# A hybrid attention, recurrence and expert layer: output projection by token block, an earlier first and second choice of experts

## The chip, the core and the metric

One core of a Trainium2 chip runs the whole layer once. The metric is the device time of one execution in microseconds (us). The engines are TensorE (PE, with its weight loads as PEld), VectorE (DVE), ScalarE (ACT), GpSimd (POOL) and the queue engine SyncE (SP). Sixteen DMA engines move data between HBM and the on-chip memory. A kernel is a list of instructions for each engine; engines meet at semaphores, and each engine runs its own list strictly in order.

## The reference

All numbers are 32-bit. There are 256 tokens of width 2048 (`SEQ`, `D_MODEL`), one layer.

```
h = x * (1.0 + scale1) + shift1
y = hybrid_mixer(h, ...)      # attention || gated recurrence, merged by gates, then @ w_out
x = layer_norm(DEEPNORM_ALPHA * x + (1.0 + gate1) * y, ln1_g, ln1_b)
h = x * (1.0 + scale2) + shift2
y = peer_ffn(h, peer_wq, peer_subkeys, peer_u, peer_v)
x = layer_norm(DEEPNORM_ALPHA * x + (1.0 + gate2) * y, ln2_g, ln2_b)

# peer_ffn, per token and head (8 heads):
q = h @ w_q;  half_scores = q . sub_keys           # two halves of 128 keys
s_top, i_top = top_k(half_scores, 16)              # then the best 16 of the 16 x 16 sums
act = x . u_tab[expert];  w = softmax(best) * gelu(act);  out = sum w * v_tab[expert]
```

So each token needs, in each of 8 heads, 16 rows of `u_tab` and 16 rows of `v_tab` (8 KB each) that depend on its own data.

## The kernel before

**Data.** Tokens are in two blocks of 128 (block 0, block 1). Weights come in chunks of 256 columns, [128, 4096] numbers (2048 KB), into four slots of `arena` called `ring[0..3]`. `stream` loads them in a fixed rotation on SP's queue. PSUM has eight banks.

**Until the output projection.** Attention, the recurrence and eight rounds of merging gates run on PE from the start to about 844 us. The last round leaves `merged_t`, the input of the output projection.

**Output projection (L884 with `merged_t`).** For each of eight weight chunks, PE multiplies both token blocks (64 recorded matmuls a chunk). Between chunks it broadcasts the adaLN rows (`spread_mod_rows`, L1039, L1035). DVE adds each finished chunk into `xr` (L1430, L1433), then takes the moments of both blocks (L1440, L1445), and normalises block 0 (L1452) while ACT normalises block 1. The columns of shift2 and scale2 go through HBM and one transpose (`mod2`, L1053).

**First choice.** PE turns block 0 (`turn`, L1063), makes the query of head 0 of block 0 (`query_of_first`, L1079) and its key scores (L1092). DVE picks the 16 experts in four pieces (`choice`, L1481 to L1534; it ends with `s_ex`). The residual rows are multiplied and shifted by the first norm's gain and bias on DVE (L1467, L1468), stored to HBM (L427) and read back much later as `xq`.

**Gathering.** Head n = 0..15 stands for block n // 8, head n % 8; step (n, e) is its row e of 16. POOL issues one indirect DMA for each (n, e): 128 tokens' rows of `u_tab` into a ring of five slots (`U_RING`) and, one head behind, of `v_tab` into a second ring of five. Experts of the last 32 key rows are not gathered (the indices past the bound are skipped); they are computed densely, 32 tiles of `dense_u` (L1141) and 32 of `v_tab` (L1153), whose tiles SP loads. DVE multiplies a gathered U row with `h2` and sums (L1561); ACT makes gelu (L716, L755), DVE the weights (`weigh`, L1572, ends with `s_wgt`), PE adds the V row (`weigh_row`, L1119).

**What sets the order.** Everything is a hand-written order. On PE, heads 1 to 7 of the query projection (L1195) have V rows of n = 0 between their quarters only from head 5 on; then steps (n, e) from (1, 12). On DVE, `choice_steps` says after which row a piece of the next choice stands: (0,4), (0,6), (0,8), (0,10), then 56 pieces over the 64 steps of n = 1 to 4. From n = 5 to n = 8 PE also spreads the gates of four tokens a step (`spread_gates`, L1179), with masks by ACT (L779) and DVE (L1626, L1634), in batches of 16 tokens (`BATCH`). `BEFORE_MASKS` = 20 dense U tiles stand before n = 5, the other 12 beside the masks. POOL's order is U(n, e), V(n-1, e), U(n, e+1), and so on; before U(n, 0) it waits for choice n.

Of the kernel before, what the change touches and what calls it, by code (L numbers as in the profile page):

```python
# [28 lines left out]
ds = bass.ds  # L29
# [21 lines left out]
BATCH = 512 // DENSE  # L51
# [17 lines left out]
QUERY_ORDER = tuple(4 * (2 * i + c) + k for i in range(2) for k in range(4) for c in range(2))  # L69
V_BANKS, V_SLOTS, V_TURNS = (7, 2, 2, 2), (0, 1, 1, 2), (0, 0, 1, 1)  # L70
# [77 lines left out]
def block_kernel(nc, consts, x_rows, x_t, cond_cols, ada_early, ada_late, bias_cols, bias_late, w_early, weights, lb_logits, norm_gain,  # L148
                 ln_cols, ln_rows, subkeys_t, expert_u, expert_v, dense_u, x_mid, mod2, out):
    with ExitStack() as ctx:  # L150
# [15 lines left out]
        ring = [arena[:, s * CHUNK:(s + 1) * CHUNK].rearrange("p (k n) -> p k n", k=KT) for s in range(4)]  # L166
# [6 lines left out]
        ln1 = arena[:, 4 * CHUNK:5 * CHUNK].rearrange("p (a n) -> p a n", a=2)  # L173

# [4 lines left out]
        merged_t = buf_b[:].rearrange("p (k t) -> p k t", k=KT)  # L179
# [145 lines left out]
        s_ea, s_eb, s_a, s_am, s_bm = sem1("ga_exp"), sem1("gb_exp"), sem("branch_a"), sem1("a_merged"), sem1("b_merged")  # L325
        s_mm, s_row, s_mg = sem("mod_row_products"), sem1("mod_rows_ready"), sem1("merged_ready")
        s_xr, s_ln, s_sk = sem("x_rows_loaded"), [sem("ln1_loaded"), sem("ln2_loaded")], sem("subkeys_loaded")
        s_modst, s_modl, s_mcol, s_colp = sem("mod_row_stored"), sem("mod_rows_loaded"), sem("mod2_cols_turned"), sem("norm_cols_ready")
        s_x1, s_mid, s_xq = sem("x_mid_ready"), [sem("x_mid0_stored"), sem("x_mid1_stored")], sem("x_quads_loaded")
# [28 lines left out]

        def wait_for_row(engine, row):

            engine.wait_ge(u_used[row % U_RING], 2 + row // U_RING)


        def v_place(n, e):

            row = n * TOPK + e
            if n < BLOCKS * HEADS - 1:
                return v_slot[row % V_RING], v_used[row % V_RING], v_loaded[row % V_RING], row // V_RING
            if e % 2 == 0:
                row = n * TOPK + e // 2  # L370
                return v_slot[row % V_RING], v_used[row % V_RING], v_loaded[row % V_RING], row // V_RING
            row = (n + 1) * TOPK + e // 2
            return u_slot[row % U_RING], u_used[row % U_RING], u_loaded[row % U_RING], row // U_RING
# [5 lines left out]
        F_QUERY = tuple(n + 2 for n in F_OUT)  # L379
# [3 lines left out]
        FIRST_BESIDE = 12  # L383
        row_order = [(n, e) for n in range(BLOCKS * HEADS) for e in range(TOPK)]
        choice_steps = row_order[4:12:2] + [row_order[TOPK + i * 64 // 56] for i in range(56)]
        dense_steps = [row_order[TOPK + FIRST_BESIDE + 1:5 * TOPK], row_order[5 * TOPK:9 * TOPK - 4]]
        mask_steps = [(n, e) for n in range(FIRST_MASKS, HEADS + 1) for e in range(TOPK)]
        v_steps = row_order[10 * TOPK - 3:16 * TOPK - 3]
# [11 lines left out]
        SOFT_AT = {choice_steps[4 * k - 2]: k for k in range(4, BLOCKS * HEADS)}  # L400
        BATCHES_OF_HEADS = [(0, 0, 1), (0, 1, 4), (0, 4, HEADS), (1, 0, HEADS)]
        QUADS_AT = {choice_steps[11]: ("experts", 1), choice_steps[14]: ("gates", 1), choice_steps[27]: ("experts", 2),
                    choice_steps[30]: ("gates", 2), (5, 1): ("experts", 3), (5, 2): ("gates", 3)}
        ACT_DELAY, MIX_DELAY = 2, 6
# [7 lines left out]
        for step in row_order[:row_order.index((HEADS, TOPK - 1)) + 1]:  # L412
            if step in mask_steps and mask_steps.index(step) >= MIX_DELAY and mask_steps.index(step) % 4 == MIX_DELAY % 4:
# [17 lines left out]
        def _(sp):  # L431
# [67 lines left out]
            for a in range(2, DENSE):  # L499
                load_v_tile(a)  # L500
# [1269 lines left out]
```

## Time and profile before

| | us |
|---|---|
| median of 3 runs | 2225.26 |
| lowest, highest | 2222.92, 2225.37 |
| the profiled execution, own time | 2222.43 |
| its span in the profile | 2220.7 |
| busy: PE | 1924.0 (87%) |
| busy: DVE | 1353.3 (61%) |
| busy: POOL | 796.8 (36%) |
| busy: ACT | 385.3 (17%) |
| moved by DMA | 722.47 MB |

The profile comes from one execution. Busy shares are means over stages that have different limits, so the table by itself names no bound; a view by time does. "DMA share" is the mean busy share of the 16 DMA engines in a stretch, and GB/s what they moved.

### The profile page before, as it was taken

To read this page: it belongs to the slowest core of one execution; us is meant where nothing else is said; L and a number is where in the kernel's file an instruction comes from. 1 tells how busy PE (TensorE), PEld (TensorE's weight loads), DVE (VectorE), ACT (ScalarE), POOL (GpSimd) and SP (SyncE) were. 2 spreads that over 40 slices of the span, in tenths; PEclk is the share of its full clock that TensorE was granted. 3 is DMA by queue.
4 is the path that set the end of the run, shared out by engine and by line. 5 is a ranking of instruction groups with operands and counts; after the bars stand their busy time and mean duration, and the time that the engine had idled before them with its cause. 6 is when DMAs were issued, how large, how long until landed. Compare 5 with 4: busy or idle time off the path is not lost.

```text
span 2220.7 us, 27840 instructions
## 1 busy us (share of the span) xinstructions
PE 1924.0 (87%) x10667; PEld 1310.0 (59%) x10667; DVE 1353.3 (61%) x2003; ACT 385.3 (17%) x1010; POOL 796.8 (36%) x556
## 2 busy tenths in 40 slices
PE   4899999999999999989788788988975778778776
PEld 4788788888888888878555455555640112112221
DVE  7832377886544541157698898767865544454547
ACT  0122222211000000022132212644430000000001
POOL 1000000000000000014565545776877765656653
PEclk9999999999999999999899999888985888998987
DMA  9973456675765746429899999999999999999997
GB/s 386 423 309 114 155 232 256 264 302 221 284 255 228 278 179 256 160 70 357 329 392 416 409 412 411 405 401 403 386 405 379 405 416 414 402 406 414 400 393 284
DMA packets 104462, 722.47 MB, mean 325 GB/s; under 512 B 29949, under 2 KB 29981, under 8 KB 32045
## 3 DMA queue, kind: packets, MB, share of 16 engines
q0 software_dynamic: 78832, 465.61, 52.7%
q1 hardware_dynamic: 25522, 255.45, 28.8%
q8 instruction: 65, 1.06, 0.2%
q14 instruction: 43, 0.35, 0.0%
HBM read 858.38 MB, written 4.21 MB: 388 GB/s over the span
## 4 chain that ended last, share of the span: by engine, by line
PE 48%; DMA 31%; DVE 8%; issue 7%; POOL 3%; ACT 1%; SPq 0%; POOLq 0%; DVEq 0%
PE ps L876 24%; DMA arena<-expert_v,expert_q 14%; DMA arena<-expert_u,expert 12%; PE ps L884 10%; PE ps L900 4%; PE ps L1119 3%; POOL arena L535 3%; DMA mod_rows<-expert_v,expert_q 2%; DVE work L1561 2%; DMA mod_rows<-expert_u,expert 2%; PE ps L1153 2%; PE ps L1141 1%; PE ps L990 1%; DMA arena<-ada_early 1%; DVE buf_a L1561 1%
## 5 line engine op out<-in xcount | busy, mean ns | idle before, releaser
L1561 DVE CUSTOM_DVE_ANT_0 work<-arena,buf_b 128x2048 f32<-128x2048 f32 x166 | 380.9, 2294 | 266.9 <-DMA arena<-expert_u,expert 266.5
L876 PE MATMUL ps<-buf_a,arena 128*128 128x256 f32 x1920 | 418.5, 379 | 0.9 <-ACT arena L618 0.9
L1119 PE MATMUL ps<-arena,mod_rows 128*32 128x512 f32 x1648 | 254.1, 697 | 188.3 <-DMA arena<-expert_v,expert_q 153.0
L535 POOL DMA_INDIRECT arena<-expert_v,expert_q x206 | 351.7, 1707 | 171.0 <-PE ps L1119 106.9
L876 PEld LDWEIGHTS ps<-buf_a,arena 128*128 128x128 f32 x1920 | 363.5, 190 | 49.9 <-issue 1.2
L535 POOL DMA_INDIRECT arena<-expert_u,expert x205 | 274.7, 1340 | 180.0 <-DVE work L1561 84.4
L523 POOL DMA_DIRECT2D arena<-ada_late x32 | 16.9, 529 | 744.6 <-DVE mod_rows L1313 614.3
L1141 PE MATMUL ps<-arena 128*128 128x256 f32 x1024 | 267.9, 413 | 5.5 <-DMA arena<-dense_u 5.5
L1141 PEld LDWEIGHTS ps<-arena 128*128 128x128 f32 x1024 | 200.0, 203 | 122.2 <-issue 88.6
L1119 PEld LDWEIGHTS ps<-arena,mod_rows 128*32 128x32 f32 x1648 | 38.3, 115 | 300.5 <-DMA arena<-expert_v,expert_q 223.3
L716 ACT ACTIVATE work<-work 32x4 f32<-32x4 f32 (+3 forms) x320 | 66.4, 207 | 556.5 <-DVE work L1561 549.1
L1313 DVE SCALAR_TENSOR_TENSOR mod_rows<-arena,cols,mod_rows 128x4096 f32<-128x4096 f32 x32 | 143.4, 4481 | 13.5 <-DMA arena<-ada_late 10.4
L1153 PE MATMUL ps<-arena 128*32 128x512 f32 x1024 | 133.8, 657 | 0.0
L1561 DVE CUSTOM_DVE_ANT_0 work<-mod_rows,buf_b 128x2048 f32<-128x2048 f32 x42 | 96.4, 2294 | 57.9 <-DMA mod_rows<-expert_u,expert 57.8
L1153 PE MATMUL ps<-arena,buf_a 128*32 128x512 f32 x1024 | 131.2, 646 | 0.0
L884 PE MATMUL ps<-arena,buf_a 128*128 128x256 f32 x512 | 112.3, 379 | 0.0
L876 PE MATMUL ps<-arena 128*128 128x256 f32 x512 | 111.8, 379 | 0.0
L884 PE MATMUL ps<-arena,buf_b 128*128 128x256 f32 x512 | 111.7, 379 | 0.0
L884 PEld LDWEIGHTS ps<-arena,buf_b 128*128 128x128 f32 x512 | 97.1, 190 | 15.7 <-issue 2.8
L900 PE MATMUL ps<-buf_a,arena 128*128 128x256 f32 x384 | 94.7, 411 | 12.3 <-ACT buf_a L591 12.3
L876 PEld LDWEIGHTS ps<-arena 128*128 128x128 f32 x512 | 97.3, 190 | 13.2
L884 PEld LDWEIGHTS ps<-arena,buf_a 128*128 128x128 f32 x512 | 96.9, 190 | 13.0
(256 smaller groups left out, 2078.7 us busy)
## 6 DMA issues: line engine op xcount, KB each, us to landing
arena<-weights SPq DMA_DIRECT2D x62, 2048.0 KB, 8.5
arena<-ada_late POOLq DMA_DIRECT2D x32, 2048.0 KB, 10.4
arena<-ada_early SPq DMA_DIRECT2D x16, 2048.0 KB, 16.9
arena<-dense_u SPq DMA_DIRECT2D x32, 1024.0 KB
arena<-expert_v SPq DMA_DIRECT2D x32, 1024.0 KB
arena<-w_early SPq DMA_DIRECT2D x8, 1536.0 KB, 8.6
arena<-expert_v,expert_q POOLq DMA_INDIRECT x206, 18.3
arena<-expert_u,expert POOLq DMA_INDIRECT x205, 18.3
```

The source lines that it names most:

```text
L523: pool.dma_start(ada_slot[s], ada_late[ds((i * 2 + s) * P, P), g * ADA_COLS:(g + 1) * ADA_COLS])\
L535: pool.indirect_dma_start(slot, None, table, bass.IndirectOffsetOnAxis(ap=indices[:, n // HEADS, column:column + 1], axis=0), bounds_check ...
L716: last = run(target(k, g), source(k, g), function)
L876: last = mm(ps[:, bank, c * TOKENS:(c + 1) * TOKENS], ring[slot][:, first + k, c * P:(c + 1) * P], rhs[:, k, :], start=(k == 0), stop=(k = ...
L884: last = mm(ps[:, bank, b * COLS:(b + 1) * COLS], lhs[:, k, b * P:(b + 1) * P], ring[slot][:, k, :], start=(k == 0), stop=(k == KT - 1))
L900: last = mm(ps[:, c // 2, c % 2 * TOKENS:(c % 2 + 1) * TOKENS], early_slot[g % 2][:, k, c * P:(c + 1) * P], h_t[:, 2 * g + k, :], start=fi ...
L990: last = mm(ps[:, bank + n // 4, n % 4 * P:(n % 4 + 1) * P], decay[:, n, m], decay[:, n, m], start=True, stop=True)
L1119: last = mm(ps[j * GROUP:(j + 1) * GROUP, n // HEADS * QUADS + g, :], spread_w[n % 2][:, e, :], slot[:, j * QCOLS:(j + 1) * QCOLS], start= ...
L1141: last = mm(ps[:, 4 + a % 2, 0:TOKENS], tile[:, k, :], h2_t[:, k, :], start=k == 0, stop=k == KT - 1)
L1153: last = mm(ps[j * GROUP:(j + 1) * GROUP, r, :], dense_act[a // 16][:, a % 16, r * GROUP:(r + 1) * GROUP], dense_slot[t % 2][:, j * QCOLS: ...
L1313: v.scalar_tensor_tensor(out=sums, in0=ada_slot[s], scalar=cond[:, ds(k, 1)], in1=sums, op0=ALU.mult, op1=ALU.add).then_inc(ada_used[s], 1)
L1561: v.tensor_tensor_reduce(out=products[n], in0=u_slot[s], in1=h2[:, n // HEADS], scale=1.0, scalar=0.0, op0=ALU.mult, op1=ALU.add, accum_ou ...
```

## The change

What it does, in the kernel's names:

- **By token block.** `out_product(j)`: eight chunks for block 0 (`FIRST_OUT`), its norm, turn, query and first choice, then eight chunks for block 1 (`SECOND_OUT`) one by one, with `add_out(j)` on DVE between the U rows of n = 0 (`out_steps`). The ring has six slots. Block 1 uses chunks 4, 5, 6, 7 and 3 as they lie; chunks 2, 0 and 1 are loaded a second time.
- **shift2 and scale2** become columns by 32 products with one column of ones (`mod2_cols`, L1105), and no longer by eight row broadcasts and HBM.
- **The rings start short.** U rows 0 to 7 turn over three slots. U row 8 waits for product 13 (`s_om`), V rows 0 and 2 for products 14 and 15.
- **Choices.** The order of choices is 0, 1, 8, 9, 2, 3, ... (`CHOICE_ORDER`). Head 1 of block 0 has its query between products 12 and 13; choice 1 stands after rows (0,12) to (0,15). One piece follows each row from (1,4) to (4,11).
- **Block 1** is normalised after row (0,15), turned, and has its queries of heads 0 and 1 on PE with V rows (0,0) to (0,3) around the second. Heads 2 to 7 then have a V row after every quarter.
- **Masks** in batches of 8 tokens; `BEFORE_MASKS` = 14, so 18 dense U tiles stand beside the masks. Dense V tiles start at step (9,4), not (9,13).
- **Norm 1's gain and bias** are applied to `xq` at n = 12 (four passes on DVE) from 0.5 MB more of `ln_rows`; the 2 MB load of them before is gone, and so are the four passes L1467, L1468.
- **U sums:** the product of a row goes back onto its own slot; DVE waits for the row before it only at e = 15.

```diff
+FIRST_OUT = ((0, 0, 1), (1, 1, 1), (2, 2, 1), (3, 3, 1), (4, 4, 1), (5, 5, 1), (6, 1, 2), (7, 2, 2))
+SECOND_OUT = ((4, 4, 1), (5, 5, 1), (6, 1, 2), (7, 2, 2), (3, 3, 1), (2, 5, 2), (0, 2, 3), (1, 3, 2))
+        U_ORDER = [(0, 1, U_RING - 1)[row % 3] if row < TOPK // 2 else (row - 1) % U_RING for row in range(BLOCKS * HEADS * TOPK + TOPK)]
-        choice_steps = row_order[4:12:2] + [row_order[TOPK + i * 64 // 56] for i in range(56)]
+        CHOICE_ORDER = [0, 1, HEADS, HEADS + 1] + list(range(2, HEADS)) + list(range(HEADS + 2, BLOCKS * HEADS))
+        choice_steps = row_order[12:16] + row_order[TOPK + 4:TOPK + 60]
+        out_steps = {(0, 0): 9, (0, 2): 10, (0, 4): 11, (0, 7): 12, (0, 11): 13, (0, 14): 14, (0, 15): 15}
-        BEFORE_MASKS = 20
+        BEFORE_MASKS = 14
...
+            pool.wait_ge(s_xn[0], 1)
             store_residual(pool, 0)
             wait_alone(pool, s_ex, 1)
+            wait_alone(pool, s_om, GATES + 1)
             for e in range(TOPK):
+                if e == TOPK // 2:
+                    wait_alone(pool, s_om, GATES + 6)
                 gather_u(0, e)
...
             for n in range(1, BLOCKS * HEADS):
-                wait_alone(pool, s_ex, n + 1)
+                wait_alone(pool, s_ex, AFTER_CHOICE[n])
...
+            for h in range(2, HEADS):
+                query_head(h)
                 if h == 3:
+                    gelu(1)
+                if h < HEADS - 1:
+                    soft_exp(h)
...
+                for k in range(KT):
+                    last = mm(ps[:, j % 4, 0:COLS], merged_t[:, b, k, :], ring[s][:, k, :], start=k == 0, stop=k == KT - 1)
+                last.then_inc(s_om, 1)
...
-                if row:
-                    dve.wait_ge(u_used[(row - 1) % U_RING], 2 + (row - 1) // U_RING)
-                v.tensor_tensor_reduce(out=products[n], in0=u_slot[s], in1=h2[:, n // HEADS], scale=1.0, scalar=0.0,
+                v.tensor_tensor_reduce(out=slot, in0=slot, in1=h2[:, n // HEADS], scale=1.0, scalar=0.0,
```

PE from the last broadcast ahead of the output projection to the first choice's scores. Before (`arena,buf_b` is a weight chunk times `merged_t`; `cst,buf_a` is the turn of a block; L1092 are scores):

```order
L884 MATMUL ps<-arena,buf_b 128x256 x32
L1053 MATMUL ps<-cst,work 128x32
L884 MATMUL ps<-arena,buf_b 128x256 x96
L1063 MATMUL ps<-cst,buf_a 128x128 x16
L1079 MATMUL ps<-arena 128x256 x16
L1063 MATMUL ps<-cst,buf_a 128x128 x8
L1086 MATMUL ps<-cst,work 128x128 x2
L1063 MATMUL ps<-cst,buf_a 128x128 x8
L1092 MATMUL ps<-work 128x128 x2
```

Now (L1120 the products, L1138 the turn, L1157 a query, L1175 scores):

```order
L1120 MATMUL ps<-arena,buf_b 128x256 x128
L1099 MATMUL ps<-mod_rows,cst 32x512 x4
L1105 MATMUL ps<-cols,mod_rows 128x1 x16
L1138 MATMUL ps<-cst,buf_a 128x128 x16
L1157 MATMUL ps<-arena 128x256 x16
L1145 MATMUL ps<-cst,arena 128x128 x8
L1165 MATMUL ps<-cst,mod_rows 128x128 x2
L1145 MATMUL ps<-cst,arena 128x128 x8
L1175 MATMUL ps<-work 128x128 x2
L1120 MATMUL ps<-arena,buf_b 128x256 x80
L1157 MATMUL ps<-arena 128x256 x16
```

The turn of block 0 stood behind all 256 products; it now stands behind 128 of them, and the 128 of block 1 come after the scores of the first choice.

POOL around the end of U(1, 15) and the start of U(2, 0), now (`experts_ready` is `s_ex`):

```order
L570 DMA mod_rows<-expert_u,expert 128x2048 [waits u4_used]
L570 DMA arena<-expert_v,expert_q 128x2048 [waits v0_used]
L570 DMA arena<-expert_u,expert 128x2048 [waits u0_used]
L570 DMA arena<-expert_u,expert 128x2048 [waits experts_ready,u1_used]
L570 DMA arena<-expert_v,expert_q 128x2048 [waits experts_in_quads,v1_used]
```

DVE there, now: the last part of choice 2 (L1615 to L1620 ends with `s_ex`) after row (1, 15) (L1645 is a U row):

```order
L1645 ISA arena,work<-arena,buf_b 128x2048
L1645 ISA work 128x1
L1615 TENSOR_TENSOR work<-work 128x256 x2
L1617 TENSOR_REDUCE cst<-work 128x2x16
L1618 SCALAR_TENSOR_TENSOR work<-cst 128x16
L1620 CAST expert<-work 128x16
```

POOL's order is as before; the choice that U(2, 0) waits for stood some twelve rows earlier on DVE and now ends behind the last row of the head before it.

## Rows read from the trace of the kernel before

**Rows 1.** Windows (start:end, length, busy, clock, DMA share, GB/s).

```profile
core 0: us, PE busy (x) PEld busy (x) DVE busy (x) ACT busy (x) POOL busy (x), PEclk, DMA share, GB/s
844.00:1100.00 256.00, 235.60 (x1105) 195.41 (x1104) 113.45 (x239) 43.53 (x119) 56.28 (x38) 0.96 0.58 219
...
1145.00:1385.00 240.00, 203.00 (x1030) 126.13 (x1029) 210.10 (x526) 55.28 (x137) 134.29 (x99) 0.97 1.01 412
1385.00:1670.00 285.00, 241.34 (x1420) 160.49 (x1418) 206.72 (x338) 136.22 (x399) 212.54 (x130) 0.88 1.00 401
1670.00:2177.00 507.00, 381.92 (x2936) 94.24 (x2936) 261.92 (x238) 19.67 (x96) 329.04 (x220) 0.85 1.00 401
```

**Rows 2.** The page's DMA issues: a weight chunk.

```profile
arena<-weights SPq DMA_DIRECT2D x62, 2048.0 KB, 8.5
```

**Rows 3.** PE timeline (start, us, what): column products; one weight chunk's products.

```profile
98.40 0.95 PE L893 MATMUL ps<-cols,work 128*128 128x1 f32 x8
...
847.02 13.98 PE L884 MATMUL ps<-arena,buf_b 128*128 128x256 f32 x64
```

**Rows 4.** Timeline, from the last product to the first gather.

```profile
966.25 0.75 DVE L1430 SCALAR_TENSOR_TENSOR work<-mod_rows,ps 128x256 f32<-128x256 f32 x2 [12.34 <-PE ps L884]
...
971.44 3.68 PE L1063 MATMUL ps<-cst,buf_a 128*128 128x128 f32 x16 [5.23 <-DVE buf_a L1452]
...
985.12 0.48 DVE L1481 MAX8 work<-work 128x8 f32<-128x128 f32 x2
...
994.47 0.17 DVE L1534 CAST expert<-work 128x16 uint32<-128x16 f32 x1
...
995.65 2.17 POOL L535 DMA_INDIRECT arena<-expert_u,expert  x1 [12.95 <-DVE expert L1534]
```

**Rows 5.** DVE timeline: U rows 0, 15, 16, 32, 34, 38, 44, 80, 144.

```profile
1004.14 2.29 DVE L1561 CUSTOM_DVE_ANT_0 buf_b<-arena,buf_b 128x2048 f32<-128x2048 f32 x1 [4.94 <-DMA arena<-expert_u,expert]
...
1056.57 2.29 DVE L1561 CUSTOM_DVE_ANT_0 buf_b<-arena,buf_b 128x2048 f32<-128x2048 f32 x1
...
1073.30 2.29 DVE L1561 CUSTOM_DVE_ANT_0 buf_a<-arena,buf_b 128x2048 f32<-128x2048 f32 x1 [14.44 <-DMA arena<-expert_u,expert]
...
1148.00 2.29 DVE L1561 CUSTOM_DVE_ANT_0 buf_a<-arena,buf_b 128x2048 f32<-128x2048 f32 x1
...
1157.63 2.29 DVE L1561 CUSTOM_DVE_ANT_0 buf_a<-mod_rows,buf_b 128x2048 f32<-128x2048 f32 x1
...
1177.03 2.29 DVE L1561 CUSTOM_DVE_ANT_0 buf_a<-arena,buf_b 128x2048 f32<-128x2048 f32 x1
...
1208.69 2.29 DVE L1561 CUSTOM_DVE_ANT_0 buf_a<-mod_rows,buf_b 128x2048 f32<-128x2048 f32 x1 [1.31 <-DMA mod_rows<-expert_u,expert]
...
1384.73 2.29 DVE L1561 CUSTOM_DVE_ANT_0 work<-arena,buf_b 128x2048 f32<-128x2048 f32 x1
...
1670.15 2.29 DVE L1561 CUSTOM_DVE_ANT_0 work<-mod_rows,buf_b 128x2048 f32<-128x2048 f32 x1
```

**Rows 6.** PE timeline: quarters of a query head, a V row between.

```profile
1099.07 3.72 PE L1195 MATMUL ps<-arena 128*128 128x256 f32 x16
1102.72 1.06 PE L1119 MATMUL ps<-arena,mod_rows 128*32 128x512 f32 x8
1103.72 3.72 PE L1195 MATMUL ps<-arena 128*128 128x256 f32 x16
```

**Rows 7.** Window of ten us after a stall of PE.

```profile
1060.00:1070.00 10.00, 6.78 (x34) 6.55 (x35) 0.00 (x0) 5.81 (x19) 4.96 (x5) 0.66 1.01 423
```

**Rows 8.** Groups and waits beside the masks, 1395 to 1655 us (61 steps).

```profile
L1141 PE MATMUL ps<-arena 128*128 128x256 f32 x384 | 110.3, 437 | 0.0
...
PE ps L1119 <- DMA arena<-expert_v,expert_q: 22.7, 15, 4.4
...
DVE work L1561 <- DMA arena<-expert_u,expert: 50.6, 34, 3.9
```

More of the change, by code:

```diff
@@ L357, in wait_alone, with u_place, v_expert @@
             engine.nop(nofuse=True)
+        U_ORDER = [(0, 1, U_RING - 1)[row % 3] if row < TOPK // 2 else (row - 1) % U_RING for row in range(BLOCKS * HEADS * TOPK + TOPK)]
+        def u_place(row):
+            s = U_ORDER[row]
+            return u_slot[s], u_used[s], u_loaded[s], U_ORDER[:row].count(s)
         def wait_for_row(engine, row):
-            engine.wait_ge(u_used[row % U_RING], 2 + row // U_RING)
+            _, slot_used, _, turn = u_place(row)
+            engine.wait_ge(slot_used, 2 + turn)
+        FIRST_OF_BANKS = [q * QUADS for q in range(QUADS)]
+        def v_expert(n, e):
+            return (FIRST_OF_BANKS + [x for x in range(TOPK) if x % QUADS])[e] if n == HEADS else e
         def v_place(n, e):
@@ L683, in _ @@
                 run(ln_rstd[b], ln_log[b], ACT.Exp, scale=-0.5).then_inc(s_std, 1)
[L684 to L687 removed]
+            rstd_of_block(0)
             act_e.wait_ge(s_colp, 1)
@@ L843, in _, with first_query_rows, first_pq @@
-            for n in range(1, BLOCKS * HEADS):
+            def first_query_rows(u):
+                act_e.wait_ge(s_q0, u + 1)
+                run(first_query, ps[:, 6 + UNITS[u][0], 0:2 * P], ACT.Copy).then_inc(s_q0r, 1)
+            def first_pq(u):
+                h, b = UNITS[u]
+                act_e.wait_ge(s_q0t, u + 1)
+                run(pq_t[h].rearrange("p (c t) -> p c t", c=2)[:, :, b * P:(b + 1) * P],
+                    ps[:, 6 + h, 2 * P:4 * P].rearrange("p (c t) -> p c t", c=2), ACT.Copy).then_inc(s_pq0, 1)
@@ new lines, in first_keep, with query_head @@
+            def first_keep(u, signal):
+                act_e.wait_ge(s_ks0, u + 1)
+                keep(*UNITS[u], slice(0, 2)).then_inc(signal, 1)
+            def query_head(h):
+                s = h % 2
+                act_e.wait_ge(used[s], 1 + F_QUERY[s] + h // 2 + 1)
+                run(pq_t[s], ps[:, 6 + s, :], ACT.Copy).then_inc(s_pq, 1)
+                act_e.wait_ge(s_ks, h - 1)
+                for b in range(BLOCKS):
+                    last = keep(h, b, slice(0, 2))
+                last.then_inc(s_kept, 1)
@@ new lines, in _ @@
+            first_query_rows(0)
+            h2_rows(0, (0, 1))
+            first_pq(0)
+            h2_rows(0, (2, 3))
+            act_e.wait_ge(s_mid[0], 16 * QUADS)
+            first_keep(0, s_first)
+            soft_exp(0)
+            experts_to_quads(0)
+            first_query_rows(1)
+            first_pq(1)
+            first_keep(1, s_first)
+            gates_to_quads(0)
+            soft_exp(1)
+            rstd_of_block(1)
+            act_e.wait_ge(s_std, BLOCKS)
+            me.link(run(ln_log[1], ln_mv[1][:, 0:1], ACT.Copy, scale=-1.0))
@@ L1107, in _ @@
-            turn_back(0, (0, 1))
+            score_first(0)
+            for j in range(GATES, GATES + 5):
+                out_product(j)
+            query_rows(1)
             turn_query(1)
-            turn_back(0, (2, 3))
-            pe.wait_ge(s_pq, 1)
-            score_first(1).then_inc(s_ks, 1)
+            out_product(GATES + 5)
+            score_first(1)
+            out_product(GATES + 6)
+            out_product(GATES + 7)
+            pe.wait_ge(s_h2, TURNED)
+            turn(1, range(TURNED))
@@ L1122, in weigh_row @@
                 last.then_inc(slot_used, 1)
+            pe.wait_ge(s_wgt, 1)
+            pe.wait_ge(s_h2, TURNED + 1)
+            for e in range(2):
+                weigh_row(0, e)
+            query_rows(3)
+            turn_query(3)
+            for e in range(2, QUADS):
+                weigh_row(0, e)
+            score_first(3)
             def turn_stats(turn, groups):
@@ L1188, in score_half @@
                 return last
-            for h in range(1, HEADS):
+            for h in range(2, HEADS):
                 s = h % 2
-                pe.wait_ge(loaded[s], (F_QUERY[s] + h // 2 + 1) * 16)
+                pe.wait_ge(loaded[s], (F_OUT[s] + 2 + s + h // 2) * 16)
                 for i in range(4):
```

434 lines of the change are left out of this document (222 added, 212 removed).

## The prediction

> **What bounds the kernel now.** The windows by time come first. From 1145 us to 2177 us the DMA share is 1.00 or 1.01 in each of three stages, while PE, the busiest engine, is at 75 to 85% of them [rows 1]. That second half is bound by bytes. From 844 us (the last merging round) to 1100 us the share is 0.58 [rows 1], so the DMA engines lie idle for 0.42 x 256 = 108 us. The reader should see a ledger in this: the end is 844 us, plus the transfers still owed, plus the idle time among them. A change moves the end only by adding or removing bytes, or by idle DMA time. The timeline says why the idle time is there: all of the output projection stands ahead of the norm, and the first gather goes out at 995.65 us [rows 4].
>
> **Prices.** A weight chunk is 2048 KB [rows 2], 2.10 MB, at 412 GB/s [rows 1] 5.1 us. A gathered row: from 1670 to 2177 us, 507 us at 401 GB/s are 203 MB [rows 1]; 30 dense tiles of 1.05 MB leave 172 MB for 224 rows (U and V of seven heads), 0.77 MB or 1.9 us. PE: both blocks of a chunk take 13.98 us [rows 3], one block 7.0.
>
> **Output projection of block 0.** The eight broadcasts leave it; 16 column products come ahead of it, 32 records at 0.95/8 us [rows 3], 3.8 us on PE's path, so it begins at 851 us and ends at 851 + 8 x 7.0 = 907 us. The last product's sum to the turn takes 5.2 us now [rows 4]; PE has 16 more column products and the spread of gate2 (5 us) there, so the turn starts at about 912. From turn to choice is 13.7 us and the choice 9.5 [rows 4]; I add 1.5 us for two turns back and two row copies put between. First gather: 936 us against 995.65, 60 us sooner.
>
> **Its rows do not flow at once.** I go through the ledger of DMA time.
> - 844 to 907: six chunks, one query chunk, subkeys: 38 us of work, 24 idle.
> - 907 to 936: norm, query, choice. Only the residual store, 2.5 us: 27 idle.
> - 936 to 975: U rows 0 to 7 on three slots, and four chunks: 15 + 20 us, 4 idle. PE does products 8 to 12 (35 us from 925), the query of head 1 (7), and product 13, to about 975. U row 8 waits for that.
> - 975 to 1003: eight U rows and five V rows, 25 us, 3 idle. U row 8 lands 8.5 us after its issue, as now (995.65 to 1004.14 [rows 4, 5]); rows 12 to 15 each have a piece of choice 1 (2.4 us), so choice 1 ends near 1014 us.
> - 1003 to 1044: until 1015 nothing may be gathered. Block 1's norm, turn and query hold PE from 1016 to 1044, with V rows 0 to 3 in it, and V slots free up late. Nine rows, one store, one chunk: 25 us, 16 idle. U row (1,0) is reduced at about 1025 (now 1073.30 [rows 5]).
> - 1044 to 1094: heads 2 and 3 of the query take 4 x 4.65 + 1 = 19.6 us each with their V rows (the pitch of [rows 6]). 18 rows and three chunks are 50 us: none idle.
> - 1094 to 1101: U row (2,0) needs choice 2, which now ends behind row (1,15). POOL stands at that wait, and every V gather behind it. The rings run dry: 7 idle.
>
> That is 81 us idle, against 108: **27 us less**.
>
> **What is owed.** Three chunks are loaded twice: +15.3 us. Norm 1's quads, 0.5 MB: +1.3. The 2 MB load that goes away was made before 844 us beside work and gives nothing. So 27 - 17 = 10 to 11 us of gain. The Trainium skill ("DMA: Bandwidth & Descriptors", section Bandwidth) says that for HBM to SBUF transfers a limit of about 358 GB/s per core binds; the rows show 401 to 412 here, so the trace disagrees; by 358 the three chunks would cost 17.6 us, and the gain would be some 2 us smaller.
>
> **Edits that I cost at small or nothing.** The four residual passes (DVE, 2.3 us each) leave a stretch where DVE waits anyway, and return at n = 12, where DVE is busy 262 of 507 us [rows 1]: nothing. U sums onto the row and one wait less a row: DVE's rows already follow each other without a gap; nothing, at best 0.1 us a row on an engine that isn't the bound. V rows in another order at n = 8 and dense V from (9,4): the same bytes; nothing, with PE at 75% for cover. Column products for HBM: mod2's 32 KB: nothing. ACT has head 3's copy behind the exponential of choice 2, which waits for row (1,14); PE then waits some 10 us for that copy at about 1083, and so on at each head, so the query ends near 1186 us and not 1134. The dense U tiles start that much later; DMA has rows to carry meanwhile, so I count nothing, and it is a rival below.
>
> **Clock.** PE will stand idle some 25 us before block 1's turn. After such a stall of its own the kernel shows 0.66 granted in ten us [rows 7], half speed for most of them: about 5 us more on the query of block 1, of which I count 2 as idle DMA.
>
> **DVE beside choices.** One piece a row instead of 7 in 8. Four rows with four pieces take 1177.03 - 1157.63 = 19.4 us [rows 5], 4.85 a row; the pitch from (2,0) to (5,0) is (1384.73 - 1148.00)/48 = 4.93 [rows 5]. They just fit: 0 to 3 us; I take 0.
>
> **Beside the masks.** Six more tiles, 24 pieces over 60 steps, 0.4 a step. A piece is 110.3/48 = 2.3 us [rows 8], so PE gains 0.9 us a step on 241/64 = 3.8 [rows 1]: 4.7. DMA gains 0.4 x 0.26 MB, 0.26 us, on (1670.15 - 1384.73)/64 = 4.46 [rows 5]: 4.7. The two are level. PE now waits 22.7 us in 61 steps for V rows and DVE 50.6 for U rows [rows 8]. If PE's waits can't shrink, 60 x 0.35 = 21 us are lost; if they do, none. I take 2, being nearer the end where buffers of five rows cover it.
>
> **Sum.** 2222.4 (the profiled execution) - 11 + 2 + 2 = 2215.4 us. The median of the runs is 2.8 us above that execution, so **2218 us**, some 7 us or 0.3% faster.
>
> **Rivals.**
> 1. *The gap closes further.* Products 13 to 15 and choice 1 come as above, but block 1's stretch (16 idle) and choice 2's (7) are filled, because rows already queued cover them. Then 11 + 12 = 23 us of gain: 2202. For it: at 1060 to 1070 the share is 1.01 although PE is busy 6.8 of 10 us [rows 7], so queued rows do cover gaps of that size. Against: POOL's waits stand in program order.
> 2. *Given back.* The late query holds back V rows and the dense tiles, and PE must catch up in n = 2 to 4. Some 10 us of idle DMA appear after 1101: about 2226, no change. For it: PE and DVE are both within 10% of DMA's pace there.
> 3. *Slower: PE becomes the bound beside the masks.* Batches of 8 make PE and DVE meet every second step instead of every fourth. The point from which it decides is a step over 4.7 + 0.18 = 4.9 us (11 us over 60 steps eat the gain). At 5.05 to 5.1 the loss is 22 us: 2238.
> 4. *It doesn't start early.* If products of block 1 wait for DVE's sums, which stand behind U rows, U row 8 comes 15 us later and choice 1 with it: 2230.
>
> **How the numbers follow.** Forecast (2212 to 2220) 0.36; rival 1 (up to 13 us or more beyond) 0.22; rival 2 (2221 to 2230) 0.20; rival 3 0.15; rival 4 0.07. What a measurement of this kernel can tell from no change is about 0.2%, 4.5 us. Faster: 0.36 + 0.22 = 0.58; same 0.20; slower 0.22. The range leaves one in ten at each side: 2202, rival 1's centre, to 2235, inside rival 3.
>
> **What would show it.** In the new profile: first gather near 936; U row 8's issue near 975; (1,0) near 1025; a DMA gap of about 7 us between (1,15) and (2,0); (5,0) some 15 to 25 us sooner than 1384.73 (fewer dense tiles are behind it); a step of 4.7 us between (5,0) and (9,0); DMA share 1.0 from (2,0) on. The prediction is wrong if the share falls under 0.97 anywhere after (2,0), or if idle DMA from 844 to 1100 is not 75 to 90 us.

## The result, and the profile after

| | before | after |
|---|---|---|
| median of 4 runs each | 2224.09 us | 2242.04 us |
| lowest, highest | 2222.76, 2225.37 | 2239.43, 2247.84 |
| profiled execution, span | 2222.43, 2220.7 | 2239.43, 2237.8 |
| moved by DMA | 722.47 MB | 727.16 MB |

The ratio is 1.0084, 95% interval 1.0070 to 1.0098: the change makes the kernel 0.8% slower. The forecast was 2218 us, and the range ended at 2235. The sign and the size were both wrong.

Read the windows by time first, as before the change. The columns are the same as in [rows 1].

```profile
core 0: us, PE busy (x) PEld busy (x) DVE busy (x) ACT busy (x) POOL busy (x), PEclk, DMA share, GB/s
906.00:936.00 30.00, 29.98 (x169) 26.31 (x168) 15.63 (x55) 9.03 (x23) 2.23 (x4) 0.94 0.14 36
...
1003.00:1044.00 41.00, 27.16 (x149) 21.48 (x150) 30.84 (x63) 19.37 (x58) 13.37 (x11) 0.78 0.77 288
1044.00:1100.00 56.00, 38.57 (x193) 26.00 (x191) 38.48 (x107) 8.11 (x38) 21.77 (x17) 0.85 0.75 294
844.00:1100.00 256.00, 210.00 (x1046) 172.50 (x1044) 137.01 (x309) 42.72 (x138) 69.01 (x52) 0.91 0.68 263
1100.00:1145.00 45.00, 25.69 (x117) 18.74 (x118) 27.16 (x68) 8.56 (x26) 13.14 (x11) 0.76 0.79 315
1145.00:1385.00 240.00, 205.66 (x1037) 132.16 (x1036) 194.01 (x500) 53.08 (x159) 129.87 (x95) 0.95 0.93 371
1385.00:1670.00 285.00, 263.06 (x1583) 186.65 (x1581) 206.41 (x393) 131.48 (x381) 188.23 (x124) 0.96 1.00 403
1670.00:2177.00 507.00, 375.20 (x2877) 96.94 (x2880) 267.81 (x245) 23.88 (x115) 352.37 (x219) 0.86 1.01 404
```

From 844 to 1100 us the share rose from 0.58 [rows 1] to 0.68: 82 us of idle DMA time instead of 108. The forecast had 81. But 1145 to 1385 us, where it stood at 1.01 [rows 1], is now at 0.93, and 1100 to 1145 at 0.79. That is 17 and 9 us of new idle time. So the 26 us that the early start gained were given back between 1100 and 1385 us, and the bytes owed came on top. From 1385 us on, the queues are as full as before.

The U rows on DVE tell the same in order of time: rows 0, 8, 16, 31, 32, 80 and 144, beside [rows 5].

```profile
942.16 2.29 DVE L1645 CUSTOM_DVE_ANT_0 arena<-arena,buf_b 128x2048 f32<-128x2048 f32 x1 [6.03 <-DMA arena<-expert_u,expert]
...
981.62 2.29 DVE L1645 CUSTOM_DVE_ANT_0 arena<-arena,buf_b 128x2048 f32<-128x2048 f32 x1
...
1022.70 2.29 DVE L1645 CUSTOM_DVE_ANT_0 arena<-arena,buf_b 128x2048 f32<-128x2048 f32 x1 [2.14 <-DMA arena<-expert_u,expert]
...
1111.42 2.29 DVE L1645 CUSTOM_DVE_ANT_0 arena<-arena,buf_b 128x2048 f32<-128x2048 f32 x1 [6.04 <-DMA arena<-expert_u,expert]
...
1121.95 2.29 DVE L1645 CUSTOM_DVE_ANT_0 arena<-arena,buf_b 128x2048 f32<-128x2048 f32 x1 [6.41 <-DMA arena<-expert_u,expert]
...
1384.37 2.29 DVE L1645 CUSTOM_DVE_ANT_0 mod_rows<-mod_rows,buf_b 128x2048 f32<-128x2048 f32 x1 [2.53 <-DMA mod_rows<-expert_u,expert]
...
1688.19 2.29 DVE L1645 CUSTOM_DVE_ANT_0 arena<-arena,buf_b 128x2048 f32<-128x2048 f32 x1
```

The first row comes 62 us sooner than before, row (1,0) 51 us, row (2,0) 26 us, and row (5,0) 0.4 us. The lead melts between (1,0) and (5,0). At (5,0) six dense tiles fewer have been moved than before. They are moved by (9,0), which is 18 us late, and the end is 17 us late. The forecast had (5,0) 15 to 25 us sooner.

**Where it melts.** Here are the waits from 1044 to 1240 us: engine and line, what it waited for, us in total, times, longest.

```profile
PE ps L1287 <- ACT work L856: 46.9, 4, 17.0
...
ACT mod_rows L741 <- DVE mod_rows L1606: 124.2, 7, 23.8
...
POOL arena L570 <- PE ps L1210: 63.6, 15, 21.9
...
POOL arena L570 <- DVE expert L1620: 16.7, 1, 16.7
```

L1287 is the key scores of a query head on PE. L856 is ACT's copy of that head's query. L741 is ACT's exponential of a choice (`soft_exp`), L1606 the end of the third piece's work on DVE, L1210 a V row on PE, L570 POOL's gathers, and L1620 the end of a choice. One turn of it is in the timeline (start, us, what, idle time before it and who ended it), on ACT, then PE, then POOL:

```profile
1077.00 0.22 ACT L741 ACTIVATE mod_rows<-mod_rows 128x16 f32<-128x16 f32 x1 [14.65 <-DVE mod_rows L1606]
1077.12 0.58 ACT L856 ACTIVATE work<-ps 128x512 f32<-128x512 f32 x1
...
1056.07 3.72 PE L1296 MATMUL ps<-arena 128*128 128x256 f32 x16
1059.72 1.06 PE L1210 MATMUL ps<-arena,mod_rows 128*32 128x512 f32 x8
1077.75 2.07 PE L1287 MATMUL ps<-work 128*128 128x128 f32 x8 [16.96 <-ACT work L856]
...
1079.62 4.98 PE L1296 MATMUL ps<-arena 128*128 128x256 f32 x16
...
1086.46 0.99 POOL L570 DMA_INDIRECT arena<-expert_v,expert_q  x1 [21.94 <-PE ps L1210]
...
1116.43 0.99 POOL L570 DMA_INDIRECT arena<-expert_u,expert  x1 [16.66 <-DVE expert L1620]
```

PE has finished head 2's last quarter at 1059.8 us, and the V row behind it at 1060.8. The copy that it needs takes 0.58 us, but in ACT's program it stands behind the exponential of choice 9, and that waits until 1077.00 for a piece which DVE works off one a U row. Meanwhile PE stands still for 17 us, with four more V rows behind the scores. No V slot comes free, POOL stands 21.94 us at a V gather, and the U gathers that stand behind it don't go out. DVE then has no U rows, and with them no place for the next piece: a row there waits 7.96 us for its bytes, and the exponential behind it (choice 2) comes at 1104.32.

```profile
1095.33 2.29 DVE L1645 CUSTOM_DVE_ANT_0 arena<-arena,buf_b 128x2048 f32<-128x2048 f32 x1 [7.96 <-DMA arena<-expert_u,expert]
...
1104.32 0.22 ACT L741 ACTIVATE mod_rows<-mod_rows 128x16 f32<-128x16 f32 x1 [23.80 <-DVE mod_rows L1606]
```

The wait feeds what it waits for: **a ring, ACT to PE to POOL to DMA to DVE and back to ACT**. In [rows 5] nothing of the kind held the rows, and in the kernel before, from 966 to 1140 us, ACT's exponentials waited for nothing. ACT's longest waits for the copies were for PE, which had not yet finished a head, and PE waited 9.8 us for the copies:

```profile
ACT work L822 <- PE ps L1195: 91.8, 6, 23.9
...
PE ps L1186 <- ACT work L822: 9.8, 4, 7.8
```

The Trainium skill ("PSUM — Partial Sum Buffer", section Engine vs sequencer instructions) says that the queues of ScalarE, VectorE and GpSimd are "strict FIFO". The trace agrees: the copy starts 0.12 us after the start of the exponential ahead of it and not before, though its input had been ready since 1059.8 us.

There are two candidates for the time, both of which come from choices that are late. One is the ring. The other is the single wait of POOL for choice 2 (16.66 us at 1116.43). Both needed experiments.

### The profile page after: what moved, and what is told of

The parts are those of the page before. It is cut to its first block, busy times and chain, and to the rows that moved or that the text cites. A ratio compares the mean times of both kernels' runs of the same rounds, so it can differ in the third digit from the quotient of the medians.

```text
span 2237.8 us, 27901 instructions
## 1 busy us (share of the span) xinstructions
PE 1910.5 (85%) x10718; PEld 1315.5 (59%) x10718; DVE 1361.2 (61%) x2079; ACT 378.2 (17%) x1036; POOL 803.1 (36%) x555
## 2 busy tenths in 40 slices
DMA packets 105020, 727.16 MB, mean 325 GB/s; under 512 B 30028, under 2 KB 30028, under 8 KB 32348
## 4 chain that ended last, share of the span: by engine, by line
PE 48%; DMA 32%; DVE 9%; issue 5%; POOL 4%; ACT 1%; SPq 0%; POOLq 0%; DVEq 0%
PE ps L937 23%; DMA arena<-expert_v,expert_q 14%; DMA arena<-expert_u,expert 9%; DMA mod_rows<-expert_u,expert 7%; PE ps L945 5%; PE ps L1120 4%; POOL arena L570 3%; DVE arena L1645 3%; PE ps L961 3%; PE ps L1210 2%; PE ps L1296 2%; PE ps L1242 2%; DMA arena<-ada_early 2%; PE ps L1157 1%; PE ps L1051 1%
## 5 line engine op out<-in xcount | busy, mean ns | idle before, releaser
L1645 DVE CUSTOM_DVE_ANT_0 arena<-arena,buf_b 128x2048 f32<-128x2048 f32 x204 | 467.4, 2292 | 332.1 <-DMA arena<-expert_u,expert 331.0
L570 POOL DMA_INDIRECT arena<-expert_v,expert_q x206 | 347.5, 1687 | 198.5 <-PE ps L1210 125.6
L1210 PE MATMUL ps<-arena,mod_rows 128*32 128x512 f32 x1648 | 241.1, 663 | 159.9 <-DMA arena<-expert_v,expert_q 137.2
L570 POOL DMA_INDIRECT arena<-expert_u,expert x204 | 271.6, 1331 | 226.2 <-DVE work L1645 101.6
L1242 PE MATMUL ps<-arena 128*128 128x256 f32 x1024 | 258.0, 402 | 3.8 <-DMA arena<-dense_u 3.8
L1242 PEld LDWEIGHTS ps<-arena 128*128 128x128 f32 x1024 | 194.6, 197 | 111.4 <-issue 80.5
L1210 PEld LDWEIGHTS ps<-arena,mod_rows 128*32 128x32 f32 x1648 | 38.3, 114 | 269.9 <-DMA arena<-expert_v,expert_q 208.5
L1645 DVE CUSTOM_DVE_ANT_0 mod_rows<-mod_rows,buf_b 128x2048 f32<-128x2048 f32 x52 | 119.4, 2297 | 75.8 <-DMA mod_rows<-expert_u,expert 75.6
L755 ACT ACTIVATE work<-work 32x4 f32<-32x4 f32 (+2 forms) x336 | 69.5, 207 | 551.8 <-DVE work L1645 515.9
L937 PE MATMUL ps<-arena 128*128 128x256 f32 x512 | 111.8, 379 | 0.0
L1120 PE MATMUL ps<-arena,buf_b 128*128 128x256 f32 x512 | 111.2, 379 | 0.0
L570 POOL DMA_INDIRECT mod_rows<-expert_v,expert_q x50 | 86.1, 1723 | 65.7 <-PE ps L1210 44.2
L937 PEld LDWEIGHTS ps<-arena 128*128 128x128 f32 x512 | 97.3, 190 | 13.2
L1120 PEld LDWEIGHTS ps<-arena,buf_b 128*128 128x128 f32 x512 | 97.0, 190 | 13.0
```

The lines of the kernel that those rows point to most:

```text
L570: pool.indirect_dma_start(slot, None, table, bass.IndirectOffsetOnAxis(ap=indices[:, n // HEADS, column:column + 1], axis=0), bounds_check ...
L755: last = run(target(k, g), source(k, g), function)
L937: last = mm(ps[:, bank, c * TOKENS:(c + 1) * TOKENS], ring[slot][:, first + k, c * P:(c + 1) * P], rhs[:, k, :], start=(k == 0), stop=(k = ...
L1120: last = mm(ps[:, j % 4, 0:COLS], merged_t[:, b, k, :], ring[s][:, k, :], start=k == 0, stop=k == KT - 1)
L1210: last = mm(ps[j * GROUP:(j + 1) * GROUP, n // HEADS * QUADS + g, :], spread_w[n % 2][:, e, :], slot[:, j * QCOLS:(j + 1) * QCOLS], start= ...
L1242: last = mm(ps[:, 4 + a % 2, 0:TOKENS], tile[:, k, :], h2_t[:, k, :], start=k == 0, stop=k == KT - 1)
```

## The experiments

Each variant is an edit of the changed kernel unless it says otherwise. All were timed beside the kernel before, at 2223.0 to 2223.8 us. A ledger over all versions follows them.

### Exponentials behind the next head's copy

```
             gates_to_quads(1)
-            soft_exp(HEADS + 1)
             for h in range(2, HEADS):
                 query_head(h)
-                if h == 3:
+                if h == 4:
                     gelu(1)
+                soft_exp(h - 1 if h > 2 else HEADS + 1)
                 if h == 5:
                     experts_to_quads(2)
-                if h < HEADS - 1:
-                    soft_exp(h)
-                if h == 5:
+                if h == 6:
                     gates_to_quads(2)
```

> Edit to the changed kernel: on ScalarE each exponential of a choice stands one query head later, behind the copy of the next head (it was ahead of it), and the gelu of the second slot stands behind head 4. Theory A, a ring of waits (ScalarE waits for the choice's third piece, TensorE for ScalarE's copy, GpSimd for TensorE's V slot, the gathers for GpSimd, VectorE for the gathers, and so the choice): the 47 us in which TensorE stood still at the ends of the heads (16.96, 5.54, 14.24, 10.18) nearly vanish, the DMA idle time between 1044 and 1385, 40 us in the changed kernel, falls by 20 to 27, and the time to 2215 to 2223 us. Rival B, the wait for choice 2 (the gathers of slot 2 wait for its last piece, 16.66 us of GpSimd on VectorE): that wait stays, the heads end earlier, and the time falls by less than 5 us, to 2237 or more.

Measured: 2205.62 us (2204.27 to 2206.82), ratio to before 0.9919 (0.990 to 0.9938). The same two waits, and ACT's timeline:

```profile
PE ps L1285 <- ACT work L856: 2.9, 2, 2.6
...
POOL arena L570 <- DVE expert L1618: 21.9, 1, 21.9
...
1063.81 0.60 ACT L856 ACTIVATE work<-ps 128x512 f32<-128x512 f32 x1
...
1078.37 0.22 ACT L741 ACTIVATE mod_rows<-mod_rows 128x16 f32<-128x16 f32 x1 [12.05 <-DVE mod_rows L1604]
1084.74 0.60 ACT L856 ACTIVATE work<-ps 128x512 f32<-128x512 f32 x1 [6.16 <-PE ps L1294]
```

The exponential still waits 12 us for DVE, but the copy of the next head is no longer behind it in time: it is PE now that ACT waits for. PE's 46.9 us are 2.9. Not one U row's work or one choice's place was changed, and 36 us are gone, more than the 19 to 27 expected. POOL's wait for choice 2 even grew to 21.9 us, so that wait is not what made the change slower than the kernel before; what it costs is read below. By program order DVE doesn't need the exponential of a choice before the second piece of the next choice, whose first piece already needs the next head's scores. The edit also moves `gelu(1)` and `gates_to_quads(2)` one head later, which this run doesn't separate; PE now waits 12.13 us at 1121.85 for the weights of U rows (1,0) to (1,15), a wait that the changed kernel doesn't show between 1044 and 1240 us.

This run also shows that there is feedback. The exponential of choice 9 comes at 1077.00 in the changed kernel and at 1078.37 here, so the first stall of 17 us is not the ring's work: the choice is simply late. From there the changed kernel falls behind although the pieces stand in the same places: choice 2 at 1104.32 against 1100.06, choice 3 at 1140.33 against 1130.58, choice 7 at 1240.77 against 1208.15. The lag is 4, 10 and 33 us. The last pair's lines, the changed kernel's and then this run's:

```profile
1240.77 0.21 ACT L741 ACTIVATE mod_rows<-mod_rows 128x16 f32<-128x16 f32 x1 [5.25 <-DVE mod_rows L1606]
```

```profile
1208.15 0.22 ACT L741 ACTIVATE mod_rows<-mod_rows 128x16 f32<-128x16 f32 x1 [7.31 <-DVE mod_rows L1604]
```

### Pieces three rows earlier, both edits, and one row earlier

```
-        choice_steps = row_order[12:16] + row_order[TOPK + 4:TOPK + 60]
+        choice_steps = row_order[12:16] + row_order[TOPK + 1:TOPK + 57]
```

> Edit to the changed kernel: the choices' pieces from the third choice on stand three U rows earlier (from row (1,1) instead of (1,4)). Theory A (the ring): the exponentials are released three rows earlier too, at 6 us a row some of the 47 us of TensorE's standstill goes, 3 to 8 us of time, to 2234 to 2239. Rival B (the wait for choice 2): GpSimd's 16.66 us are gone, and 10 to 15 us of time with them, 2227 to 2232. Nothing at all would say that the choices bound neither.

Measured: 2197.14 us (2191.47 to 2198.02), ratio 0.9876 (0.9853 to 0.9899). This is far more than either expectation.

> Both edits: exponentials behind the next head's copy, and pieces three rows earlier. If ring and choice wait are two costs, the gains add: 2205 to 2215 us, DMA idle time between 1044 and 1385 under 12 us. If one of them was the whole cost, this equals that one alone within 2 us.

Measured: 2194.81 us (2192.32 to 2198.95), ratio 0.9869 (0.9849 to 0.9888). The gains are 36, 45 and together 47 us, so they don't add: this is 2.3 us under the three rows alone, inside the spread, and far under the 2205 to 2215 of two separate costs.

> Edit to the changed kernel: pieces from the third choice on one U row earlier (e2 had three). If each row of lateness counts alike, a third of e2's 45 us: 2222 to 2230. If the ring snaps (a feedback in which a small lead is enough), most of it: 2200 to 2210.

Measured: 2216.69 us (2212.85 to 2221.46), ratio 0.9971 (0.9959 to 0.9983). That lies between the two expectations, and decides for neither. PE's wait for ACT's copies and POOL's for a choice, from 1044 to 1240 us, of one row earlier, of three rows earlier, and POOL's of both edits together:

```profile
PE ps L1287 <- ACT work L856: 23.4, 4, 10.0
...
POOL arena L570 <- DVE expert L1620: 5.6, 1, 5.6
```

```profile
PE ps L1287 <- ACT work L856: 8.2, 3, 5.6
...
POOL arena L570 <- DVE expert L1620: 6.5, 1, 6.5
```

```profile
POOL arena L570 <- DVE expert L1618: 9.7, 1, 9.7
```

With rows 0, 1 and 3 earlier, PE waits 46.9, 23.4 and 8.2 us, and the time is 2242, 2217 and 2197. One row is (1111.42 - 1022.70)/15 = 5.9 us in slot 1, and it bought 25 us. This size by itself doesn't show feedback: four late copies, each 5.9 us less late, are 23.6 us, and PE's waits fell by 23.5. POOL's wait for choice 2 fell too, from 16.7 to 5.6 us. What does show it are again the times of the exponentials. One row earlier, that of choice 9 comes 7.4 us sooner than in the changed kernel (1069.64 for 1077.00), that of choice 3 20.4 us sooner, and that of choice 6 32.4 us sooner (1181.97 for 1214.35). The lead grows from head to head, because each shorter stall lets the next piece come sooner.

Three rows earlier opens the ring without touching ACT's order, which is why the other edit adds only 2 us to it. On top of the ACT edit, the earlier pieces are worth 11 us, and POOL's wait for choice 2 falls from 21.9 to 9.7 us, which leaves no gap in the queues, as the ledger below shows. So that wait probably had its price too, at most 11 of 47 us, about a quarter; the earlier pieces move every choice, and no run takes that one wait away alone.

### One part undone: the early choices

```
-        CHOICE_ORDER = [0, 1, HEADS, HEADS + 1] + list(range(2, HEADS)) + list(range(HEADS + 2, BLOCKS * HEADS))
+        CHOICE_ORDER = list(range(BLOCKS * HEADS))
-        choice_steps = row_order[12:16] + row_order[TOPK + 4:TOPK + 60]
+        choice_steps = row_order[12:16] + row_order[TOPK + 8:TOPK + 64]
```

> Edit to the changed kernel: one part undone. Block 1's first two choices are not made early; choices 2, 3, ... of block 0 stand four U rows earlier each ((1,8) on), ScalarE's exponentials stay where they are, directly behind each head. Theory A (the choices' lateness closes the ring): it costs nothing that the two choices are late, the third pieces come four rows sooner, TensorE's waits for ScalarE's copies fall from 47 to under 12 us, 2195 to 2207 us. Rival C (the ring is closed by the V rows between the query heads whatever the order of the choices): 2225 or more.

With the order of choices, the exponentials of choices 8 and 9 also leave their place ahead of head 2's copy, and go to where those of block 1 stand, and `gates_to_quads(1)` goes behind head 2's copy. Choices 2 to 7 stand four U rows earlier each.

Measured: 2200.38 us (2194.33 to 2206.82), ratio 0.9893 (0.9875 to 0.9910), as theory A expected. PE's waits for the copies are 10.0 us:

```profile
PE ps L1286 <- ACT work L856: 10.0, 2, 9.8
```

So the part of the change that closes the ring is "two of its choices early": choices 8 and 9 stand ahead of choices 2 to 7 in DVE's order and push each of them back, and choice 9's exponential stands ahead of head 2's copy on ACT. These two are one part of the change, and this run doesn't separate them. The V rows between the query heads are a link of the ring, but with earlier pieces they are harmless (rival C falls). The variant that takes those V rows away alone wasn't tried; by program order POOL would stand at V gathers that no head frees, with the pieces for the heads behind it.

### What the second loads cost

> Edit to the changed kernel: the three column chunks that are loaded a second time are not (block 1's last three products take the chunk that lies in the slot, so the output is wrong; 6 MB less is moved). If the transfers are what the reloads cost, 3 x 5.1 = 15.3 us less, 2226 to 2229. If the queues stand idle in the stretch anyway (share .88 and .77 there), part of it is covered: 5 to 10 us, 2232 to 2237. If the reloads cost nothing, the whole +17 us comes from elsewhere, 2240 or more.

```
-SECOND_OUT = (..., (2, 5, 2), (0, 2, 3), (1, 3, 2))
+SECOND_OUT = (..., (2, 5, 1), (0, 2, 2), (1, 3, 1))
-            load_chunk(OUT0 + 2, 5, late_out_loaded[1])
...
-            load_chunk(OUT0, 2, loaded[2])
...
-            load_chunk(OUT0 + 1, 3, loaded[3])
```

Block 1's last three products take the chunk that lies in the slot, and the three chunks that belong there are not loaded.

Measured: 2246.64 us (2243.75 to 2249.38), ratio 1.0109 (1.0086 to 1.0131), nothing saved at all. The 4.6 us more are not clear of the spread, as the intervals of the two ratios overlap. The same change of the version with both edits:

> e3_both without the three second loads of column chunks (output wrong in block 1's last three products; 6 MB less). In e4 the same cut of the changed kernel gave nothing, its idle time grew by what was saved. If that was because the ring bound the time, here, where the queues are busy from 1044 on, it gives 10 to 15 us (2180 to 2185). If the reloads lie in idle time of the queues anyway (the gathers ahead of 1044 wait for choice 1, not for transfers), it gives under 4 us here too (2191 or more).

Measured: 2193.95 us (2190.78 to 2198.41), ratio 0.9880 (0.9863 to 0.9896), 0.9 us under the version with both edits, which is inside the spread. So the three loads cost nothing that these runs can tell, in either version. The time of their transfers turned up as idle time in the stretch before 1044 us. The likely reason is that the gathers there wait for choices and PE's products and not for bytes. In the window from 844 to 1044 us the share falls from 0.65 (both edits) to 0.60 without them. The 200 us lines of the two kernels:

```profile
844.00:1044.00 200.00, 170.67 (x841) 146.21 (x843) 96.40 (x210) 33.16 (x99) 44.73 (x34) 0.91 0.65 250
```

```profile
844.00:1044.00 200.00, 172.38 (x856) 147.03 (x854) 100.96 (x220) 36.23 (x109) 45.85 (x37) 0.92 0.60 229
```

### The second choice earlier as well

The edit is one of the version with both edits.

```
-        choice_steps = row_order[12:16] + row_order[TOPK + 1:TOPK + 57]
+        choice_steps = row_order[8:12] + row_order[TOPK + 1:TOPK + 57]
```

> e3_both with the second choice four U rows earlier as well (its pieces behind rows (0,8) to (0,11) instead of (0,12) to (0,15)). Its scores lie ready at 978 in e3, where the pieces start at 998. If the transfers bound everything behind 1044 and the idle queues between 975 and 1044 (5 and 9 us in e3) come from this choice (GpSimd waits 13.1 us for it at 1019), the time falls by 5 to 10 us against e3, to 2185 to 2190. If the U slots and the waits for TensorE's products hold the gathers there, it falls by under 2 us.

Measured: 2192.78 us (2191.07 to 2194.47), ratio 0.9869 (0.9852 to 0.9885): 2 us under both edits, which is inside the spread. POOL's timeline shows why. Of the version with both edits first, then of this one:

```profile
1019.03 0.98 POOL L570 DMA_INDIRECT arena<-expert_u,expert  x1 [13.10 <-DVE expert L1618]
...
1035.09 0.99 POOL L570 DMA_INDIRECT arena<-expert_v,expert_q  x1 [9.89 <-PE ps L1208]
```

```profile
1034.39 0.99 POOL L570 DMA_INDIRECT arena<-expert_v,expert_q  x1 [17.06 <-PE ps L1208]
```

The wait for the choice is gone, and the next one, for the first V slot that PE frees, is longer by 7 us. POOL goes on at 1034.4 instead of 1035.1. PE frees that slot behind the norm, the turn and the query of block 1. This is a wait that took the place of the one removed.

### The ledger over all versions

Idle DMA time is (1 - share) x length, of the windows 844 to 1044 and 1044 to 1385 us (rounding of the share makes it +-3 us). The windows of the second stretch, in order: before, after, ACT edit, one row earlier, three rows earlier:

```profile
1044.00:1385.00 341.00, 285.06 (x1442) 184.48 (x1441) 291.08 (x718) 80.06 (x218) 194.83 (x138) 0.95 0.98 395
```

```profile
1044.00:1385.00 341.00, 269.92 (x1346) 176.90 (x1345) 259.65 (x673) 69.74 (x223) 164.78 (x123) 0.90 0.88 351
```

```profile
1044.00:1385.00 341.00, 294.89 (x1529) 191.37 (x1528) 284.87 (x714) 94.34 (x300) 187.77 (x137) 0.95 0.97 395
```

```profile
1044.00:1385.00 341.00, 289.17 (x1466) 188.26 (x1466) 276.63 (x698) 89.53 (x291) 182.72 (x132) 0.93 0.95 383
```

```profile
1044.00:1385.00 341.00, 305.64 (x1597) 199.76 (x1590) 294.07 (x725) 96.85 (x310) 203.58 (x140) 0.96 1.00 406
```

| version | idle 844-1044 | idle 1044-1385 | span | span less idle |
|---|---|---|---|---|
| before | 100 | 7 | 2220.7 | 2114 |
| after | 68 | 41 | 2237.8 | 2129 |
| ACT edit (e1) | 68 | 10 | 2205.2 | 2127 |
| one row earlier (e9) | 68 | 17 | 2213.2 | 2128 |
| three rows earlier (e2) | 70 | 0 | 2195.2 | 2125 |
| both edits (e3) | 70 | 0 | 2197.2 | 2127 |
| early choices undone (e8) | 72 | 3 | 2204.8 | 2130 |
| choice 1 earlier too (e5) | 68 | -3 | 2190.5 | 2126 |
| after, no second loads (e4) | 86 | 41 | 2242.8 | 2116 |
| both edits, no second loads (e6) | 80 | -3 | 2189.0 | 2112 |

The last column is nearly a constant: 2125 to 2130 for every version with the change's bytes, 2112 and 2116 for those without the 6 MB, and 2114 before the change. The time of this kernel is that constant plus the idle DMA time. The change cuts 32 us of idle time before 1044 us, adds 34 behind it, and owes some 11 to 16 us of bytes. With the ring open some 30 us stay. This is bookkeeping: it says in which stretch the time lies, and the experiments say why.

## Why the prediction was wrong, point by point

- **The bound and the ledger: right.** The table above is the prediction's own ledger, and it closes within 5 us over ten kernels.
- **Early start: right.** First gather 936 foreseen; U row 0 reduced at 942.16. Row (1,0) near 1025 foreseen, 1022.70 measured. Share 0.14 from 906 to 936 us is 26 us idle, 27 foreseen. The sum from 844 to 1100 us came out at 82 where 81 stood. With that, rival 4 (no early start) and rival 1 (the gap closes further) both fell.
- **But the stages of that sum were not all right.** "1044 to 1094: none idle" measured 0.25 x 56 = 14 us to 1100 us, and 1003 to 1044 us measured 0.23 x 41 = 9 where 16 stood. The 7 us of choice 2 were foreseen before 1101 us; POOL's wait for it was 16.66 us and lasted until 1116. The total agreed in part by chance.
- **The step that failed** is the sentence on ACT: the copy of head 3 "behind the exponential of choice 2", PE waits "some 10 us for that copy ... and so on at each head", "DMA has rows to carry meanwhile, so I count nothing". Its first half was right in kind and total size: 1186 less 1134 are 52 us of such waits, and four measured 46.9. The longest, 16.96 us, was at head 2's copy behind the exponential of choice 9, which the prediction didn't have; head 3's was 5.54. The second half was the mistake. Rows don't keep coming while PE stands, because V rows are in PE's program behind the scores, and POOL's U gathers stand behind the V gathers that want their slots. The cover named for the stall was fed by the stalled engine. Where nothing was counted, 26 us of idle DMA time stood after 1100 us (the wait for choice 2 is in them), and with the ACT order mended 36 us went, twice the whole loss.
- **The end of the query was mis-summed beside it.** Six heads (2 to 7) at the prediction's own 19.6 us from 1044 us end at 1162 and not at 1134, so its own waits lead to 1214 and not to 1186. The last scores started at 1215.25. So the query was 28 us later than the prediction believed before any cover was asked for.
- **Rival 2, "Given back", was the mechanism**, with the right first half ("the late query holds back V rows"), and a wrong size: 10 us of idle DMA after 1101 us, and 26 measured. Its 2226 would have been 2242 with 26. The prediction priced it by the lag of the engines behind DMA's pace, and not by following the wait once around.
- **Rival 3 gave 2238, the nearest number, and is wrong.** The step beside the masks is (1688.19 - 1384.37)/64 = 4.75 us, foreseen 4.7, with the DMA share at 1.00. PE is busy 263 of 285 us there and was 241 [rows 1]; its waits shrank, as the forecast took it. A number that agrees doesn't make its mechanism right.
- **Owed bytes: the size right, their effect wrong.** 15.3 us per three chunks were counted as time. The ledger confirms 13 to 15 as transfer time (2129 less 2116, 2127 less 2112), but leaving them out saves nothing, since idle time takes their place. The reader should count such bytes either in a stretch that is full or not at all.
- **DVE beside choices: right.** One piece a row costs no pace once rows arrive. With both edits, rows (2,0) and (5,0) on DVE are below, (1341.51 - 1109.32)/48 = 4.84 us a row, where 4.93 stood before. What matters is how early a choice stands, not how dense its pieces are.

```profile
1109.32 2.29 DVE L1643 CUSTOM_DVE_ANT_0 arena<-arena,buf_b 128x2048 f32<-128x2048 f32 x1
...
1341.51 2.29 DVE L1643 CUSTOM_DVE_ANT_0 mod_rows<-mod_rows,buf_b 128x2048 f32<-128x2048 f32 x1 [2.54 <-DMA mod_rows<-expert_u,expert]
```

- **The signs of being wrong: one fired.** "Wrong if the share falls under 0.97 anywhere after (2,0)": it is 0.93 from 1145 to 1385 us. The other, idle time from 844 to 1100 us outside 75 to 90, did not: it is 82.

Of the versions run, choice 1 earlier with both edits is the fastest at 2192.78 us, 1.3% under the kernel before. The three fastest of the change's full computation lie within 5 us of each other, and these runs don't order them. What stays open is how much of the ACT edit's 36 us is the ring's feedback and how much the plain sum of four late copies. The growing lag of the exponentials shows that the feedback is there, but no run measured one stall alone.

## What to carry to other kernels

When a stall is costed at nothing because other work covers it, follow the wait once around: who feeds the cover, and does the stalled engine's program hold a buffer that it needs? An instruction that waits for a slow producer should stand on its engine as late as its first reader allows, above all never directly ahead of a copy on which the busiest engine waits. And a gain in one stretch should be checked at a marker far behind it (here row (5,0), 0.4 us sooner in spite of a start 60 us sooner) before it is believed.

## What the runs showed of the hardware that was not expected

Six megabytes of transfers in a stretch with a DMA share of 0.65 cost 0.9 us, inside the spread, in one version and nothing in another: their 15 us did not show in the time. And the stall cost PE more than its length. The quarter behind the 16.96 us stall took 4.98 us instead of 3.72 [rows 6], and the window after it shows a granted clock of 0.73, part of it at the lower of the two levels; ten us later it is 1.00.

```profile
1078.00:1086.00 8.00, 8.00 (x34) 6.06 (x35) 7.76 (x20) 0.66 (x2) 0.00 (x0) 0.73 0.02 9
1086.00:1096.00 10.00, 10.00 (x54) 6.83 (x53) 1.83 (x8) 0.00 (x0) 4.21 (x5) 1.00 0.70 216
```

The first of the two lines also shows the bottom of the ring: for 8 us the DMA share is 0.02, in a kernel that is bound by bytes.
